# Asking for projection weights and prompt bias rows from ACT's DMA queue instead of SP's

## What is computed

```python
z = xn @ w_in                    # columns: conv B | C | x | q | k | v | forget | gates
# prompt: 8 heads of 64, causal, with a decay by the forget logits
sc = q @ k.T / 8 + di[:, None] - dk[None, :]     # dk: running sum of log f, one row per head
p  = softmax(where(causal, sc, -inf));  out = p @ v
# samples: 4096 past tokens each, read from a paged cache (pages of 128 tokens)
k_past = cache_k[page_table];  v_past = cache_v[page_table]
sp = q @ k_past.T / 8 + d_new + rev;  out = softmax(...) @ v_past + own new tokens
```

## Time and profile before

| what | value |
|---|---|
| median of 3 runs | 2040.56 us (2038.02 to 2043.32) |
| the profiled execution's own time | 2035.48 us |
| its span in the trace | 2033.8 us |
| PE (TensorE) busy | 1876.1 us, 92% of the span |
| DVE / ACT / POOL busy | 832.8 / 442.9 / 250.4 us |
| DMA queue q1 (asked for by SP) | 365.30 MB, 50.1% of 16 engines |
| DMA queue q0 (asked for by POOL) | 91.13 MB, 12.6% of 16 engines |

### The profile page before, as it was taken

The page is one execution under the profiler, slowest core; times in us unless marked ns, Lnnn a source line. Parts: engine busy times, 40 slices in busy tenths (PEclk is TensorE's granted clock), DMA queues, the critical chain, the costliest instruction groups (busy, mean ns, idle before and its releaser), DMA issues.

```text
span 2033.8 us, 33501 instructions
## 1 busy us (share of the span) xinstructions
PE 1876.1 (92%) x12402; PEld 1109.1 (55%) x12402; DVE 832.8 (41%) x1867; ACT 442.9 (22%) x1021; POOL 250.4 (12%) x381
## 2 busy tenths in 40 slices
PE   6999988888999999999999898994999999999994
PEld 4677655545588868888864466543333333333331
DVE  5644477777666423333354406334111111111115
ACT  3111133434301011011111205231222222212213
POOL 0203233323100000000000000000111111111120
PEclk9999999989999999999999999997999999999997
DMA  7759999999912130210111204444999999999966
GB/s 269 260 168 348 351 355 360 357 323 344 318 51 87 46 127 11 63 52 11 63 65 63 85 1 156 145 148 174 353 382 386 378 370 375 374 371 376 368 225 261
DMA packets 208164, 458.56 MB, mean 225 GB/s; under 512 B 18722, under 2 KB 47419, under 8 KB 207619
## 3 DMA queue, kind: packets, MB, share of 16 engines
q1 hardware_dynamic: 177554, 365.30, 50.1%
q0 software_dynamic: 30448, 91.13, 12.6%
HBM read 432.44 MB, written 32.17 MB: 228 GB/s over the span
## 4 chain that ended last, share of the span: by engine, by line
PE 79%; DVE 6%; DMA 4%; issue 4%; ACT 4%; DVEq 2%; SPq 1%; POOLq 0%; POOL 0%; ACTq 0%
PE ps L1322 16%; PE ps L1632 11%; PE ps L1663 6%; PE ps L1151 6%; PE ps L1387 6%; PE ps L1643 5%; PE ps L1416 5%; PE ps L1672 3%; PE ps L1123 3%; PE ps L1166 3%; PE ps L1505 2%; PE ps L1274 2%; DMA kraw<-in_cache_k 2%; PE ps L1254 2%; DMA vpage<-in_cache_v 2%
## 5 line engine op out<-in xcount | busy, mean ns | idle before, releaser
L1632 PE MATMUL ps<-gu,xgT 128*64 128x512 f32 x1024 | 226.8, 595 | 0.9 <-ACT xgT L1983 0.9
L2166 DVE STREAM_TRANSPOSE kt<-kraw 128x1024 f32<-128x1024 f32 x128 | 151.2, 1219 | 47.1 <-DMA kraw<-in_cache_k 37.8
L1322 PE MATMUL ps<-xnT,ring 128*128 128x264 f32 x672 | 159.1, 387 | 0.6 <-DMA xnT<-xn_d 0.6
L861 POOL DMA_DIRECT2D vpage<-in_cache_v x228 | 122.8, 539 | 293.2 <-PE ps L1274 236.3
L2904 DVE TENSOR_TENSOR sig_a<-ps,sig_a 128x256 f32<-128x256 f32 x32 | 13.6, 425 | 324.6 <-ACT sig_a L1987 324.6
L1632 PEld LDWEIGHTS ps<-gu,xgT 128*64 128x64 f32 x1024 | 70.7, 137 | 131.9 <-issue 128.7
L1322 PEld LDWEIGHTS ps<-xnT,ring 128*128 128x128 f32 x672 | 127.3, 190 | 23.8 <-DMA xnT<-xn_d 1.8
L1663 PE MATMUL ps<-wd,hidT_a 128*64 128x512 f32 x512 | 118.6, 605 | 19.1 <-ACT hidT_a L1993 10.5
L1643 PE MATMUL ps<-gu,xgT 128*32 128x512 f32 x1024 | 115.8, 592 | 0.0
L1151 PE MATMUL ps<-xnT,early 128*128 128x352 f32 x320 | 101.1, 472 | 4.5 <-DVE xnT L2110 4.5
L1151 PEld LDWEIGHTS ps<-xnT,early 128*128 128x128 f32 x320 | 60.6, 194 | 38.3 <-issue 8.7
(11 more groups left out here) (446 smaller groups left out, 2907.6 us busy)
## 6 DMA issues: line engine op xcount, KB each, us to landing
kraw<-in_cache_k SPq DMA_DIRECT2D x256, 256.0 KB, 5.0
wd<-in_w_expert_down SPq DMA_DIRECT2D x31, 2048.0 KB, 21.0
gu<-in_w_expert_gate SPq DMA_DIRECT2D x30, 2048.0 KB, 20.4
gu<-in_w_expert_up SPq DMA_DIRECT2D x30, 2048.0 KB, 25.0
vpage<-in_cache_v POOLq DMA_DIRECT2D x228, 256.0 KB, 5.5
ring<-in_w_in SPq DMA_DIRECT2D x12, 1024.0 KB, 8.0
yy<-y_d SPq DMA_DIRECT2D x16, 512.0 KB, 9.9
early<-in_w_in SPq DMA_DIRECT2D x6, 1024.0 KB, 11.5
```

Of the source, the lines that this page charges most:

```text
L861: eng.dma_start(vpage[value_place(n)][:, p, :], t["cache_v"][ds(page, 1)].rearrange("a s d -> (a s) d")).then_inc(v_in[value_place(n)], 16)
L1322: last = nc.tensor.matmul(bank(R.bank(name, f, q))[:, 0:QT], weight[:, k], src[:, k, cols], start=k == 0, stop=k == HK - 1)
L1632: last = nc.tensor.matmul(bank(0)[h * BA:(h + 1) * BA, :].rearrange("p (x n) -> p x n", x=2), src[:, k, 0:BA], weight[:, k, :, h * DE // 2 ...
L2166: last = nc.vector.transpose(kt[n % 2].rearrange("p c e s -> p (c e s)")[:, x * 1024:(x + 1) * 1024], kraw[n % 2].rearrange("p c d -> p (c ...
```

## The change

All moved loads keep their source, target, size and semaphore. Twelve DMA instructions move from SP's list to ACT's: four of early weights (v and k, for both places) and eight of negk. On ACT each stands right behind ACT's copy of the last item that reads the place (early, and the first two sets of negk, which come behind copies of k items), or, for the third and fourth set, behind the first half's copy of the turned probabilities of units k = 7 and k = 15. SP no longer waits for these places. ACT's copy has waited for TensorE already, so ACT has no new wait but those on `neg_stored` and `xn_stored`.

```diff
-                if n == 7:
-                    R.made(sp, "q", 1, 1)
-                    early_load(0, O_V)
-                if n == 9:
-                    R.made(sp, "q", 3, 1)
-                    early_load(1, O_V)
-                if n == 15:
-                    R.made(sp, "v", 0, PT - 1)
-                    early_load(0, O_K)
-                if n == 24:
-                    R.made(sp, "v", 1, PT - 1)
-                    early_load(1, O_K)
-                if n == 28:
-                    R.made(sp, "k", 1, 1)
-                    sp.wait_ge(neg_stored, 16)
-                    load_negk(0)
-                if n == 35:
-                    R.made(sp, "k", 3, 1)
-                    sp.wait_ge(xn_stored, 16)
-                    load_negk(1)
-                if n == slot_after(PT):
-                    load_negk(2)
-                if n == slot_after(2 * PT):
-                    load_negk(3)
...
+            def load_weights(slot, c0):
+
+                act.dma_start(early[slot], w3(t["w_in"], c0 + slot * 256, 256)).then_inc(early_in[slot], 16)
+
+            def load_negk(hp):
+
+                for p in range(2):
+                    act.dma_start(negk[hp % 2][p], neg_d[2 * hp + p:2 * hp + p + 1, 0:SEQ].to_broadcast([P, SEQ])
+                                  ).then_inc(negk_in[hp % 2][p], 16)
+
+            def load_behind(kind, a, b):
+
+                if (kind, a, b) in (("q", 1, 1), ("q", 3, 1)):
+                    load_weights(a // 2, O_V)
+                if kind == "v" and b == PT - 1:
+                    load_weights(a, O_K)
+                if (kind, a, b) == ("k", 1, 1):
+                    act.wait_ge(neg_stored, 16)
+                    load_negk(0)
+                if (kind, a, b) == ("k", 3, 1):
+                    act.wait_ge(xn_stored, 16)
+                    load_negk(1)
+
...
+                    if p == 0 and k in (PT - 1, 2 * PT - 1):
+                        load_negk(k // PT + 2)
                 for item in items(n):
                     copy_item(*item)
+                    load_behind(*item)
```

More of the change, by code:

```diff
@@ L926, in load_rev @@
                              .unsqueeze(1).to_broadcast([4 * H, DS, SU * PAGE])).then_inc(rev_in[b % 2], 16)
[L928 to L939, removed]
             load_unit(0), load_unit(1)
```

## The result

The change makes the kernel slower by 0.5%: the ratio to before is 1.0051, 95% interval 1.0031 to 1.0071. The median is 2048.24 us (5 runs, 2042.9 to 2056.0) against 2040.56 us (5 runs as well, 2038.02 to 2043.32). The two medians are 7.7 us or 0.38% apart; the ratio is not their quotient, and its interval holds both. The execution that was profiled took 2042.9 us with a span of 2040.7, so 7.4 and 6.9 us more than the profiled one of before; its trace can therefore show about the difference of the medians.

A forecast was written before the change was run, and what follows sets the result against it. The prediction took TensorE as busy and the DMA engines as the resource that matters in the loop. Its terms summed to 0.0 us, giving 2040.5 us, own range 2037 to 2047, 8-in-10 range 2034 to 2048.

The forecast's parts named there:

- What bounds the stretch: Loop, 70 to 545 us: DMA engines matter, weights are never late; better transfer order can return 10.2 us plus clock loss.
- the sum: All terms over the loop: -0.7 + 1.4 + 1.4 - 2.3 + 0.2 = 0.0 us, ends -3.6 and +6.3.
- The term of the second negk pair: Load moved from 297.82 to about 268.4 us, against value pages late at 278.52: +1.4 us, bounds 0 and +2.9.
- the rival: Slower: with a third queue values get a third of the engines; stalls near 278.52 and 353.04, clock losses: +8.5 us, chance 0.15.
- The third pair: Negk load moved from 353.33 to 340.6 us, ahead of values late at 353.04: +1.4 us, bounds 0 and +2.9.
- The k weights of the first place: Asked for at 157.9 instead of 164.78 us; the 0.67 us stall at 186.50 may go: -0.7, bounds -0.7 and 0.
- The fourth pair: Negk load moved from 430.40 to 413.4 us, before a DMA hole; stalls at 444.14 and 451.00 go: -2.3, bounds -2.9 and 0.
- The issue on ACT: Issuing negk pairs on ACT takes 0.91 to 1.53 us and may overrun its idle time: +0.2 us, bounds 0 and +0.5.
- the signs given: Profile signs; for ACT's issue, PE's waits on ACT probT growing by more than 2 us would show it dear.
- No change: Whole kernel: whatever comes earlier is hidden by transfers or products; chance of within 0.3%: 0.72.
- the loop's stretch: Sign of a right forecast: the stretch from 70 to 545 us stays as long within 4 us.
- The rule that was cited against the change: DMAs started by different engines end on the same 16 DMA engines; several starters save only the sequencer's issue time.

The follow-up runs named there:

- The small issues: All real loads stay on SP at their old places while ACT issues twelve 4 KB copies, against the kernel before: ratio 0.9996, 2037.52 us.
- K0: Load of the k weights of the first place; moved alone to ACT at the change's place, against the kernel before: ratio 1.0004, 2041.55 us.
- the old moments: All twelve loads on ACT's queue, near the times at which SP asked for them before, against the kernel before: ratio 1.0028, 2043.65 us.
- N1: Negk load of the second head pair; moved alone to ACT at the change's place, against the kernel before: ratio 1.0016, 2041.64 us.
- N2: Negk load of the third head pair; moved alone to ACT at the change's place, against the kernel before: ratio 1.0026, 2042.41 us.
- V0: Load of the v weights of the first place; timed only in groups: with V1, K0, K1, N0 on ACT at the old moments, against before, 1.0015.
- V1: Load of the v weights of the second place; timed only in groups: with V0, K0, K1, N0 on ACT at the old moments, against before, 1.0015.
- K1: Load of the k weights of the second place; timed only in groups: with V0, V1, K0, N0 on ACT at the old moments, against before, 1.0015.
- N0: Negk load of the first head pair; timed only in groups: with V0, V1, K0, K1 on ACT at the old moments, against before, 1.0015.
- N3: Negk load of the fourth head pair; moved alone to ACT at the change's place, against the kernel before: ratio 1.0004, 2040.79 us.

## Why the prediction was wrong

**What bounds the stretch: right as far as it goes.** The DMA engines are the resource, the weights are never waited for, and SP's removed waits were worth nothing: SP now waits 136.3 us for transposed keys instead of 122.7. But the sum counted stalls alone and put the granted clock at nothing, and in the trace 6.7 of the 8.0 us are slower work.

**The term of the second negk pair: wrong by its size, and with the third pair's it decides.** The forecast took the middle of 0 and 2.9, +1.4. In the trace it cost 5.2 us between steps 28 and 31: 1.65 more standing for values, 1.2 more for DVE, and about 2.3 of slower products, which the term left out and which only the rival counted; in time, alone, 3.3 us (1.0016). Three choices failed in it. The middle was chosen because a queue of its own would take turns; but in this stretch, with DMA share 1.0, the early megabyte made PE stand for values about its own transfer time longer in either queue (3.5 to 4.9 us in six traces, 1.0 to 2.2 in eleven). It was also priced against the 0.47 us at 278.52 alone, without the 1.38 us at 271.99. And the clock behind a grown stall, named in the rival with 2.5 us, was not put into the sum's high end. With it, the high end of this term would have been +5.4, and that of the sum +8.8 instead of +6.3, so 2049.3 and beyond the range given.

**The third pair: too small as well.** +1.4 forecast; +3.6 at step 40 in the trace (+3.0 two steps on), 1.0026 or 5.3 us in time by itself. Here the clock is not what was missed: its fall at this place was there before (the 1.70 us at 353.04 in the earlier trace rows), so the rival's second loss of 2.5 us was not a new one. What makes 5.3 us of it the traces do not show.

**The k weights of the first place: wrong sign in the trace.** -0.7 forecast, +1.7 in the trace; in time, alone, not told from nothing (1.0004). The stall at 186.50 did go, for the 0.7 expected. But the step looked only at the stall that the load would leave, and not at the values that it would meet at its new moment: these, without a stall before, became 2.34 us late.

**The fourth pair: right in its signs, without the gain.** The hole is largely filled, both stalls at 444 and 451 are gone, steps 53 to 56 win 3.0 us (forecast 2.3) after steps 50 to 53 lost 2.9 at a lower clock, and the key pages asked for from 435 to 450 us land in:

```profile
DMA to landing us min/median/max: 2.8/5.1/8.2
```

against 8.7 and 12.4 us. The timing of this load alone (1.0004, 0.9990 to 1.0019) has no such gain: 2.3 us would be 0.9989, just outside the interval.

**The issue on ACT, +0.2: about right.** The small issues cost nothing. Of the signs given, waits on probT (L1216, now L1179) had 8.0 us before and have 8.8 now, well under the 2 us named. Pairs took 0.97, 1.01, 1.81 and 1.76 us; the last two are above the 1.5 expected, but PE's waits on probT just behind them, 0.95 and 1.94 us, are as long as in before.

**The forecast as a whole.** No change, 0.72, did not come; 2048.24 lies just beyond the range's 2048.0. Of the signs, the loop's stretch grew by 8.4 us instead of within 4, and the value stalls grew by 2.7 and 1.7 us, but with the clock's fall near 280, which the prediction itself gave as the sign of the slower rival; near 353 the same fall was there before. That rival, at 0.15, came true in its places and in one of its two clock losses. That its sum (2049) is so near is in part luck, since it holds a clock loss that is not new and leaves out K0's stall, the wait for DVE and the slower steps 50 to 53. Its 2.5 us come from 42 against 88 matmuls, which are not of the same shapes in the two windows; the clock of 0.50 over 5 us gives the same figure. Its mechanism is half of the truth. An effect of the third queue is seen in K0's traces and in the 1.0028 of the old moments, but N1's stall and N2's loss are there with SP's queue too.

**The rule that was cited against the change** (the Trainium skill, page "DMA: Bandwidth & Descriptors", section "SWDGE vs HWDGE vs iDMA") gives what another issuing engine saves. The runs agree that there was nothing to save. By that rule alone the same loads at the same moments should cost nothing on ACT either; 1.0028 (1.0014 to 1.0042) says that they do cost something here.

**What stays open:** what exactly makes V0, V1, K0, K1 and N0 cost 0.15% on ACT at the old moments; how much the queue adds to N1 and N2 at the new ones, and what of N2 costs 5 us; what kept the clock down from 425 to 445 us; and whether N3 gains anything.

## What to carry to other kernels

Where the DMA engines are full and a consumer is served just in time, asking for a load earlier need not be free: it can put about its whole transfer time in front of what is late already, on either queue, as the second negk pair did here. Look at what lands at the new moment, not only at what the old one held up, and price each grown stall with the clock loss behind it, after a look whether that loss is there already. Compare TensorE's busy time for the same matmuls before counting stalls: here it held most of the loss. When a change moves both the moment and the queue of a transfer, time each alone before crediting either.

## What the runs showed of the hardware that was not expected

ACT's DMA issues do not hold ACT's engine, and run ahead of it. ACT's timeline of after around the fourth negk pair, whose two DMAs stand in ACT's list behind the copies to probT that start at 420.12:

```profile
418.85 0.30 ACT L1797 ACTIVATE pnew<-snew,negmax 32x32 f32<-32x32 f32 x1
418.94 0.33 ACTq L1813 DMA_DIRECT2D negk<-neg_d  x1
419.06 0.19 ACT L1797 ACTIVATION_READ_ACCUMULATOR pnew<-snew,negmax 32x1 f32 x1
419.15 0.25 ACT L1732 ACTIVATE sraw<-ps 128x128 f32<-128x128 f32 x1
419.30 1.40 ACTq L1813 DMA_DIRECT2D negk<-neg_d  x1
419.31 0.81 ACT L1782 ACTIVATE prob<-prob,fstat 128x640 f32<-128x640 f32 x1
420.03 0.18 ACT L1782 ACTIVATION_READ_ACCUMULATOR prob<-prob,fstat 128x1 f32 x1
420.12 0.73 ACT L1732 ACTIVATE probT<-ps 128x512 f32<-128x512 f32 x2
```

The first issue starts 1.18 us before those copies, just when PE's products that they wait for end (418.18 + 0.72 = 418.90 us), and the exponential runs while the second is issued. So a DMA placed "behind a copy" on ACT is behind what the copy waits for, not behind the copy's own work. The pair at 347.09 us took 1.81 us to issue, and kstage behind it started at 349.00, released by a DMA of its own after 1.26 us.

The other surprise is how soon a stall costs the clock: with all loads on ACT at the old moments, the eight products near 280 us take 1.92 us instead of 1.06 behind a stall of only 1.17 us:

```profile
279.68 1.92 PE L1250 MATMUL ps<-vpage,sprobT 128*32 128x512 f32 x8 [1.17 <-DMA vpage<-in_cache_v]
```

Before, with 0.47 us of stall, they ran at full clock; also behind 1.38 us at 271.99 they did; in after, behind 3.60 us at 358.42, the eight ran at full clock (1.06 us) and the fall came in the window behind them (0.67). The length of a single stall does not tell when the clock goes.
